# Second mixer of a two-block network: level products of a pair one projection later, first outputs earlier, turning on other banks

## The chip, the cores and the metric

The program runs on 1 core of a Trainium2 chip. The metric is the device time of one execution in microseconds (us). The kernel before took 1179.19 us, the median of three runs (1178.02, 1179.58, 1179.19).

## What is computed

Two networks run one after the other on 256 tokens of width 1024, all in float32 (matrix products as sums of three, see below). The change lies in the second one's first mixer, HGRN2:

```python
proj = h @ w_in
q, fl, v, g = jnp.split(proj, ...)          # 1024 wide each, 8 heads of 128
q = silu(q)
log_f = logaddexp(log(lb), log1p(-lb) + log_sigmoid(fl))
k = (1.0 - lb) * sigmoid(-fl)
# per head, over the 256 tokens: S_t = diag(f_t) S_{t-1} + k_t v_t^T, o_t = S_t^T q_t
o = o * rsqrt(mean(o * o) + EPS) * norm_w   # per head
o = o.reshape(B, S, 1024) * silu(g)
return o @ w_out
```

The kernel computes the scores q_t . decay(t, s) . k_s without a scan over tokens: the 256 tokens are cut in halves, those in halves, and so on. For each of the levels (blocks of 1, 2, 4 ... 128 tokens) `qT` and `kT` are multiplied in place by products of `f`, then one product `kT^T qT` gives the scores of all block pairs of that level, and a mask picks them out.

## The kernel before

**Weights.** All weights come as units of 128 x 2048 float32 (1 MB) through a ring of three buffers (`NS = 3`). Each unit is loaded by SyncE in two halves (`raw`, L2135), ScalarE rounds a half to `whi` (L958), VectorE subtracts to get `wlo` (L1369; in the feed-forward stages GpSimd does some, L1942), and TensorE multiplies three times: `whi` by `hh`, `wlo` by `hh`, `whi` by `hl` (L495, L498, L501 for outputs with columns on partitions; L512, L515, L518 for outputs by token). Both engines split two units ahead of the one that is being multiplied (`use`, in each engine's program). A load waits for the `wlo` of the unit three before.

**The order of the work** is written out by hand: each engine has its own program (`tensor_program`, `scalar_program`, `vector_program`, `gpsimd_program`, `sync_program`), each runs strictly in order, and they meet at semaphores. A bank of PSUM is taken by `turn(key, bank)`; `full`, `evac` and `free` name the waits for it. Banks 0 to 3 go round for projections, banks 4 to 7 (`4 + side[0] % 4`) for level products and the first outputs.

**The mixer.** The heads are worked in four pairs, j = 0 to 3. Units in order: `hf` 0, `hq` 0, `hf` 1, `hq` 1, ... `hq` 3 (forget and query columns of pair j, `project_columns`), then `hv` 0, `hg` 0, `hv` 1, `hg` 1 (values and gate of half the heads, by token, each in two units or parts, `project_tokens`), then `ho`, the output product (`add_product`).
- `f_of(j)`: VectorE scales the forget columns out of PSUM (L1416), ScalarE makes `kT` and `fT` by Sigmoid (L1212, L1213), VectorE finishes them (L1757, L1760). GpSimd then multiplies up the block products `tot` (`products(j)`, L2074).
- `q_of(j)`: VectorE scales the query columns (L1416), ScalarE makes `qT` by Silu (L1218).
- A level product (j, i), i = 0 to 8, is step i of pair j. On TensorE (`level`) it is four products of 128 x 128 x 128 (L857), two for i = 8 (L852); the trace has two records for each such product. It needs the bank, and for i = 0 `kT` and `qT` of pair j, for i > 0 the scaling of step i - 1. VectorE (`level` in its program) waits for the product, scales `qT` and `kT` for the next one (L1781, L1782; L1774 for i = 0), then copies the masked scores into `Ss` (L1787, `copy_predicated`). Step 8 is copied by ScalarE into `S01` (L1224).
- Which steps stand behind which projection is a table `LEVEL` made by `advance(key, pairs)`: each call takes the next step of each pair in `pairs` that has not had all nine. All engines read the same table (`levels(*key)`).
- `outputs(g2)`: for each half of the tokens (`tt`), scores times values (L879, and L878 with `S01` for the second half) into a bank, ScalarE squares it for the mean (L1245), VectorE and GpSimd make the root (L1799, L1949), VectorE multiplies by root and gate into `og` (L1804). ScalarE has made `sgt`, the Silu of the gate (L1239), and GpSimd multiplied it by the norm's weights (L2084, `scaled_gate`, two operations of 128 x 512 for each half of the heads).
- `turn_outputs(cs)`: transposes `og` (L889) into a bank; ScalarE copies `eh` (L1253), VectorE `el` (L1811), the operands of `ho`.

Before the change `outputs(0)` stands behind the second part of `hg` 0, and `turn_outputs((0, 1))` behind the last projection, on banks 0 and 1. The second half of the last gate projection is in bank 0.

Of the kernel before, what the change touches and what calls it, by code (L numbers as in the profile page):

```python
# [72 lines left out]
def build(nc, a):  # L73
    V, A, G, T, S = nc.vector, nc.scalar, nc.gpsimd, nc.tensor, nc.sync
    vq, aq, gq, tq, sq = Waits(V), Waits(A), Waits(G), Waits(T), Waits(S)
    with ExitStack() as root:
# [3 lines left out]
        def sbuf(ctx, name, shape, dt=f32):  # L80
            return ctx.enter_context(nc.sbuf_tensor(name, shape, dt))
# [62 lines left out]
        lev = sbuf(hg, "lev", [128, 8, 128], i32)  # L144
# [211 lines left out]
        def turn(key, b, fills=1):  # L356
            fills_of[b] += fills
            turns[key] = (b, evacuations[b], fills_of[b])
            evacuations[b] += 1
            return b  # L360
# [9 lines left out]
        def evac(*key):  # L370
            b, n, _ = turns[key]
            return s_evac[b], n + 1
# [76 lines left out]
        at_level, level_no, LEVEL = [0] * 4, {}, {}  # L449

        def advance(key, pairs):
            for j in pairs:
                if at_level[j] < 9:
                    LEVEL.setdefault(key, []).append((j, at_level[j]))
                    level_no[j, at_level[j]] = len(level_no) + 1
                    at_level[j] += 1

        for j in range(1, 4):
            advance(("hf", j), range(j))
            advance(("hq", j), range(j + 1))  # L460
        for g2 in range(2):
            for name in ("hv", "hg"):
                for part in range(2):
                    advance((name, g2, part), range(4))
            while min(at_level[2 * g2:2 * g2 + 2]) < 9:
                advance(("rest", g2), range(4))

        lev_q = {ji: i + 1 for i, ji in enumerate(ji for ji in sorted(level_no, key=level_no.get) if ji[1] < 8)}

# [7 lines left out]
        def tensor_program():  # L477
# [55 lines left out]
            def project_tokens(key, e, between=None):  # L533
                bs = [turn(("tok", *key, 0), next_bank()), turn(("tok", *key, 1), next_bank(), 2)]
                for part in range(2):
                    j = unit_at[(*key, part)]
                    for t in range(2):
                        if part == 0:
                            tq.wait_ge(*free(("tok", *key, t)))
                        tok = moving(banks[bs[t]][:, :], j, t, hh, hl, range(4 * part, 4 * part + 4), 0, 512, *of_norm(e),  # L540
                                     first=part == 0, last=part == 1)
                        if t == 1 or part == 1:
                            tok.then_inc(s_full[bs[t]], 1)
                    b, _, n = turns["tok", *key, 1]
                    used[j, 0] = used[j, 1] = (s_full[b], n - 1 + part)
                    if between is not None:
                        between(part)
# [77 lines left out]
            for t in range(2):  # L625
                for c in range(2):
                    b = turn(("tr", 0, 2 * t + c), 4 + 2 * t + c)
# [9 lines left out]
            wh, wl, b = whole(whi, 0), whole(wlo, 0), turns["col", "xbc", 0][0]  # L637
# [30 lines left out]
            j = unit_at["dtf",]  # L668
            b = turn(("dtf",), next_bank())
# [15 lines left out]
            for tt in range(2):  # L685
                b = turn(("xst", tt), 4 + tt)
# [5 lines left out]
            for g in range(2):  # L692
                b = turn(("cb", g), 6 + g)
# [166 lines left out]
            def levels(*key):  # L860
                for j, i in LEVEL.get(key, []):
                    level(j, i)

            def outputs(g2):
                for tt in range(2):
                    b = turn(("oo", g2, tt), 4 + side[0] % 4 if g2 == 0 else 2 + tt)
                    side[0] += 1
                    for j in (2 * g2, 2 * g2 + 1):
                        tq.wait_ge(*evac("lev", j, 7))
                        tq.wait_ge(*evac("lev", j, 8))  # L870
                    tq.wait_ge(*evac("tok", "hv", g2, 0))
                    tq.wait_ge(*evac("tok", "hv", g2, 1))
                    tq.wait_ge(*free(("oo", g2, tt)))
                    for i in range(4):
                        hd = 4 * g2 + i
                        vs, out = slice(128 * hd, 128 * hd + 128), banks[b][:, 128 * i:128 * i + 128]
                        if tt == 1:
                            T.matmul(out, S01[:, hd, :], vt[:, 0, vs], start=True, stop=False)  # L878
                        tok = T.matmul(out, Ss[:, 2 * hd + tt, :], vt[:, tt, vs], start=tt == 0, stop=True)  # L879
                    tok.then_inc(s_full[b], 1)  # L880

            def turn_outputs(cs):
                for c in cs:
                    b = turn(("tr", 4, c), c % 2)
                    tq.wait_ge(*free(("tr", 4, c)))
                    for t in range(2):
                        tq.wait_ge(*evac("oo", c // 2, t))
                        for k in range(2):
                            tok = T.transpose(banks[b][:, 256 * k + 128 * t:256 * k + 128 * t + 128],  # L889
                                              og[:, t, 256 * c + 128 * k:256 * c + 128 * k + 128], ident[:, :])  # L890
                    tok.then_inc(s_full[b], 1)

            project_pair([("hf", 0), ("hq", 0)], 3)
            for j in range(1, 4):
                project_columns(("hf", j), 3)
                levels("hf", j)
                project_columns(("hq", j), 3)
                levels("hq", j)
            for g2 in range(2):
                for name in ("hv", "hg"):  # L900
                    project_tokens((name, g2), 3, lambda part: levels(name, g2, part))
                if g2 == 0:
                    levels("rest", 0)
                    outputs(0)
            turn_outputs((0, 1))
            levels("rest", 1)
            outputs(1)
            add_product(("ho",), 4, eh, el, *of_norm(4), 5, before_last=lambda: turn_outputs((2, 3)))
            feed_forward(1, 5, 6)
# [37 lines left out]
        def scalar_program():  # L947
# [272 lines left out]
            def levels(*key):  # L1220
                for j, i in LEVEL.get(key, []):
                    if i == 8:
                        aq.wait_ge(*full("lev", j, 8))
                        A.activation(S01[:, 2 * j:2 * j + 2, :], bank_of("lev", j, 8)[:, 0:256].rearrange("p (h t) -> p h t", h=2),  # L1224
                                     ACT.Copy).then_inc(evacuated("lev", j, 8), 1)

            def tokens_of(name, g2):
                factors = (factor(3, 0), factor(3, 1))
                sl = slice(512 * g2, 512 * g2 + 512)
                for part in range(2):  # L1230
                    use((name, g2, part))
                    levels(name, g2, part)
                for t in range(2):
                    key = ("tok", name, g2, t)
                    aq.wait_ge(*full(*key))
                    if name == "hv":
                        A.activation(vt[:, t, sl], bank_of(*key)[:, :], ACT.Copy, scale=factors[t]).then_inc(evacuated(*key), 1)
                    else:
                        A.activation(sgt[:, t, sl], bank_of(*key)[:, :], ACT.Silu, scale=factors[t]).then_inc(evacuated(*key), 1)  # L1239

            def outputs(g2):
                for tt in range(2):
                    aq.wait_ge(*full("oo", g2, tt))
                    for i in range(4):
                        t = A.activation(hn[:, tt, 512 * g2 + 128 * i:512 * g2 + 128 * i + 128], bank_of("oo", g2, tt)[:, 128 * i:128 * i + 128],  # L1245
                                         ACT.Square, accum_out=mstat[:, 8 * tt + 4 * g2 + i:8 * tt + 4 * g2 + i + 1])
                    t.then_inc(s_osq, 1)
# [15 lines left out]
            for g2 in range(2):  # L1263
                tokens_of("hv", g2)
                tokens_of("hg", g2)
                if g2 == 0:
                    levels("rest", 0)
                    outputs(0)
            turn_outputs((0, 1))
            levels("rest", 1)  # L1270
            outputs(1)
            add_product(("ho",), 4, 5, before_last=lambda: turn_outputs((2, 3)))
            feed_forward(1, 5, 6)
# [83 lines left out]
        def vector_program():  # L1357
# [432 lines left out]
            def levels(*key):  # L1790
                for j, i in LEVEL.get(key, []):
                    level(j, i)
# [33 lines left out]
            for g2 in range(2):  # L1826
                for name in ("hv", "hg"):
                    for part in range(2):
                        use((name, g2, part))
                        levels(name, g2, part)  # L1830
                if g2 == 0:
                    levels("rest", 0)
                    outputs(0)
            turn_outputs((0, 1))
            levels("rest", 1)
            outputs(1)
            add_product(("ho",), 4, 5, before_last=lambda: turn_outputs((2, 3)))
            feed_forward(1, 5, 6)
# [350 lines left out]
```

## Time and profile before

| | us |
|---|---|
| median of three runs | 1179.19 |
| the profiled execution, its own time | 1177.87 |
| its span, first to last instruction | 1176.6 |
| TensorE matmul busy | 1142.4 (97%) |
| TensorE weight load busy | 1061.1 |
| VectorE busy | 670.1 |
| ScalarE busy | 583.0 |
| GpSimd busy | 295.9 |

The engines run beside one another; busy time is summed over an engine's own instructions, and matmuls are pipelined, so that a busy TensorE need not be at its peak. The mixer in question runs from about 540 to 694 us of the span. The mean granted clock of TensorE is 0.989 of full speed.

### The profile page before, as it was taken

To read this page: it belongs to the slowest core of one execution; us is meant where nothing else is said; L and a number is where in the kernel's file an instruction comes from. 1 tells how busy PE (TensorE), PEld (TensorE's weight loads), DVE (VectorE), ACT (ScalarE), POOL (GpSimd) and SP (SyncE) were. 2 spreads that over 40 slices of the span, in tenths; PEclk is the share of its full clock that TensorE was granted. 3 is DMA by queue.
4 is the path that set the end of the run, shared out by engine and by line. 5 is a ranking of instruction groups with operands and counts; after the bars stand their busy time and mean duration, and the time that the engine had idled before them with its cause. 6 is when DMAs were issued, how large, how long until landed. Compare 5 with 4: busy or idle time off the path is not lost.

```text
span 1176.6 us, 19533 instructions
## 1 busy us (share of the span) xinstructions
PE 1142.4 (97%) x8221; PEld 1061.1 (90%) x8221; DVE 670.1 (57%) x1043; ACT 583.0 (50%) x891; POOL 295.9 (25%) x191
## 2 busy tenths in 40 slices
PE   8999999999999999999899999999999869999997
PEld 6999989999989999889898889999889858999986
DVE  6555765577656454337897556334247785533424
ACT  6546555555436644337543444444345954544432
POOL 2023100000005444512321115444500001544440
PEclk9899999999999999999999999999999989999999
DMA  8669574545646666655443447655555534756550
GB/s 261 203 206 331 151 242 125 165 144 144 205 148 194 189 191 203 197 162 179 143 150 107 125 153 226 192 184 195 197 161 169 172 96 144 226 180 193 184 195 36
DMA packets 158257, 207.89 MB, mean 177 GB/s; under 512 B 13631, under 2 KB 131545, under 8 KB 158170
## 3 DMA queue, kind: packets, MB, share of 16 engines
q1 hardware_dynamic: 154442, 193.63, 52.8%
q0 software_dynamic: 3728, 13.02, 3.3%
q8 instruction: 65, 1.06, 0.4%
q14 instruction: 22, 0.18, 0.0%
HBM read 205.53 MB, written 4.24 MB: 178 GB/s over the span
## 4 chain that ended last, share of the span: by engine, by line
PE 88%; DVE 6%; ACT 3%; issue 1%; DMA 1%; POOL 0%; SPq 0%; DVEq 0%; ACTq 0%; POOLq 0%
PE bank L495 18%; PE bank L501 18%; PE bank L498 18%; PE bank L518 9%; PE bank L515 9%; PE bank L512 9%; DVE wlo L1369 2%; PE bank L857 2%; ACT whi L958 1%; PE bank L783 1%; PE bank L793 1%; DMA area<-in_hgrn_lb 1%; PE bank L805 1%; PE bank L558 1%; DVE uc L1499 0%
## 5 line engine op out<-in xcount | busy, mean ns | idle before, releaser
L1369 DVE TENSOR_TENSOR wlo<-raw,whi 128x1024 fp32r<-128x1024 f32 (+1 forms) x281 | 346.1, 1260 | 236.1 <-ACT whi L958 235.5
L958 ACT ACTIVATE whi<-raw 128x1024 fp32r<-128x1024 f32 x368 | 365.6, 1042 | 118.2 <-PE bank L518 112.6
L495 PE MATMUL bank<-hh,whi 128*128 128x256 f32 x1792 | 287.1, 281 | 1.7 <-ACT hh L990 1.7
L1942 POOL TENSOR_TENSOR wlo<-raw,whi 128x1024 fp32r<-128x1024 f32 x87 | 223.3, 2567 | 255.9 <-ACT whi L958 255.9
L501 PE MATMUL bank<-hl,whi 128*128 128x256 f32 x1792 | 282.6, 279 | 0.0
L498 PE MATMUL bank<-hh,wlo 128*128 128x256 f32 x1792 | 282.6, 279 | 0.0
L495 PEld LDWEIGHTS bank<-hh,whi 128*128 128x128 f32 x1792 | 242.4, 188 | 6.7 <-issue 5.5
L498 PEld LDWEIGHTS bank<-hh,wlo 128*128 128x128 f32 x1792 | 241.7, 188 | 0.0
L501 PEld LDWEIGHTS bank<-hl,whi 128*128 128x128 f32 x1792 | 241.7, 188 | 0.0
L1949 POOL TENSOR_TENSOR st<-st,half 128x1 f32<-128x1 f32 x18 | 10.3, 581 | 438.3 <-DVE st L1386 413.4
L512 PE MATMUL bank<-whi,gh 128*128 128x512 f32 x264 | 81.5, 390 | 0.0
L515 PE MATMUL bank<-wlo,gh 128*128 128x512 f32 x264 | 81.3, 389 | 0.0
L518 PE MATMUL bank<-whi,gl 128*128 128x512 f32 x264 | 81.3, 389 | 0.0
L1186 ACT ACTIVATE sg<-sg 128x512 f32<-128x512 f32 x33 | 20.9, 632 | 95.6 <-DVE sg L1416 95.6
L1190 ACT ACTIVATE gh<-sg 128x512 fp32r<-128x512 f32 x33 | 20.8, 631 | 85.9 <-DVE sg L1730 85.9
L518 PEld LDWEIGHTS bank<-whi,gl 128*128 128x128 f32 x264 | 49.6, 188 | 10.4
L515 PEld LDWEIGHTS bank<-wlo,gh 128*128 128x128 f32 x264 | 49.6, 188 | 10.3
L512 PEld LDWEIGHTS bank<-whi,gh 128*128 128x128 f32 x264 | 49.2, 188 | 9.9
L1730 DVE TENSOR_TENSOR sg<-sg,bank 128x512 f32<-128x512 f32 x33 | 22.7, 687 | 57.5 <-PE bank L501 55.4
L1416 DVE TENSOR_TENSOR sg<-bank,bc_f 128x512 f32<-128x512 f32 x33 | 22.7, 688 | 43.9 <-PE bank L501 43.9
L983 ACT ACTIVATE bank<-x_sb 128x512 f32<-128x512 f32 x28 | 16.8, 599 | 57.1 <-DVE x_sb L1438 29.9
L1732 DVE TENSOR_TENSOR gl<-sg,gh 128x512 fp32r<-128x512 f32 x33 | 30.8, 932 | 23.3 <-ACT gh L1190 23.3
(306 smaller groups left out, 1281.1 us busy)
## 6 DMA issues: line engine op xcount, KB each, us to landing
raw<-in_ffn_w_in SPq DMA_DIRECT2D x88, 512.0 KB, 3.6
raw<-in_w_in SPq DMA_DIRECT2D x72, 512.0 KB, 4.7
raw<-in_ffn_w_out SPq DMA_DIRECT2D x44, 512.0 KB, 3.4
raw<-in_hgrn_w_in SPq DMA_DIRECT2D x32, 512.0 KB, 4.3
raw<-in_w_ffn_gate SPq DMA_DIRECT2D x22, 512.0 KB, 4.4
raw<-in_w_ffn_up SPq DMA_DIRECT2D x22, 512.0 KB, 4.1
raw<-in_w_ffn_down SPq DMA_DIRECT2D x22, 512.0 KB, 3.3
raw<-in_w_branch SPq DMA_DIRECT2D x16, 512.0 KB, 4.3
```

Source lines behind the costliest of these rows:

```text
L495: T.matmul(out, wh[:, i, c], xh[:, k, :], start=first and (i, k) == pairs[0], stop=False)
L498: T.matmul(out, wl[:, i, c], xh[:, k, :], start=False, stop=False)
L501: t = T.matmul(out, wh[:, i, c], xl[:, k, :], start=False, stop=last and (i, k) == pairs[-1])
L512: T.matmul(out, xh[:, k, r], wh[:, i, c], start=first and i == 0, stop=False)
L515: T.matmul(out, xh[:, k, r], wl[:, i, c], start=False, stop=False)
L518: tok = T.matmul(out, xl[:, k, r], wh[:, i, c], start=False, stop=last and i == len(ks) - 1)
L857: tok = T.matmul(banks[b][:, 128 * (2 * h + t):128 * (2 * h + t) + 128], kj[:, h, c], qj[:, h, c], start=True, stop=True)
L958: A.activation(half_of(whi, j, h), half_of(raw, j, h), ACT.Copy).then_inc(s_hi[j % NS][h], 1)
L1369: V.tensor_tensor(half_of(wlo, j, h), half_of(raw, j, h), half_of(whi, j, h).bitcast(f32), ALU.subtract).then_inc(s_lo[j % NS][h], 1)
L1416: V.tensor_tensor(dst, two(bank_of("col", *key)[:, :]), bc[:, :].rearrange("p (o t) -> p o t", o=1).broadcast_to([128, 2, 256]), ALU.mult) ...
L1732: V.tensor_tensor(gl[:, 2 * j:2 * j + 2, :], two(s), gh[:, 2 * j:2 * j + 2, :].bitcast(f32), ALU.subtract).then_inc(s_gl, 1)
L1942: G.tensor_tensor(half_of(wlo, j, 1), half_of(raw, j, 1), half_of(whi, j, 1).bitcast(f32), ALU.subtract).then_inc(s_lo[j % NS][1], 1)
```

## The change

The four parts of it: pair j's level step behind `hq` j is left out there, so that each pair j from 1 on starts one projection later; `outputs(0)` moves from behind `hg` 0 to behind the first part of `hv` 1, on all engines; the first turning goes to banks 6 and 7; what is left of the levels, one product (3,8), is issued on TensorE behind that turning, on ScalarE ahead of its copies of it. An assertion says that pairs 0 and 1 are done where the first outputs now stand.

```diff
         for j in range(1, 4):
             advance(("hf", j), range(j))
-            advance(("hq", j), range(j + 1))
+            advance(("hq", j), range(j))
         for g2 in range(2):
             for name in ("hv", "hg"):
                 for part in range(2):
                     advance((name, g2, part), range(4))
-            while min(at_level[2 * g2:2 * g2 + 2]) < 9:
-                advance(("rest", g2), range(4))
+                    assert (name, g2, part) != ("hv", 1, 0) or min(at_level[0:2]) == 9
+        while min(at_level) < 9:
+            advance(("rest",), range(4))
...
                     for j in (2 * g2, 2 * g2 + 1):
                         tq.wait_ge(*evac("lev", j, 7))
-                        tq.wait_ge(*evac("lev", j, 8))
+                        if tt == 1:
+                            tq.wait_ge(*evac("lev", j, 8))
...
-                    b = turn(("tr", 4, c), c % 2)
+                    b = turn(("tr", 4, c), 6 + c if c < 2 else c - 2)
...
+            def behind(name, g2, part):
+                levels(name, g2, part)
+                if (name, g2, part) == ("hv", 1, 0):
+                    outputs(0)
+
             for g2 in range(2):
                 for name in ("hv", "hg"):
-                    project_tokens((name, g2), 3, lambda part: levels(name, g2, part))
-                if g2 == 0:
-                    levels("rest", 0)
-                    outputs(0)
+                    project_tokens((name, g2), 3, lambda part: behind(name, g2, part))
             turn_outputs((0, 1))
-            levels("rest", 1)
+            levels("rest")
             outputs(1)
...
             for g2 in range(2):
                 tokens_of("hv", g2)
                 tokens_of("hg", g2)
-                if g2 == 0:
-                    levels("rest", 0)
-                    outputs(0)
+            levels("rest")
             turn_outputs((0, 1))
-            levels("rest", 1)
             outputs(1)
```

(The second hunk of the last pair is ScalarE's; VectorE's program changes as TensorE's does.) The level table, written as (pair, step):

| behind | before | now |
|---|---|---|
| `hf` 1 | 0,0 | 0,0 |
| `hq` 1 | 0,1 1,0 | 0,1 |
| `hf` 2 | 0,2 1,1 | 0,2 1,0 |
| `hq` 2 | 0,3 1,2 2,0 | 0,3 1,1 |
| `hf` 3 | 0,4 1,3 2,1 | 0,4 1,2 2,0 |
| `hq` 3 | 0,5 1,4 2,2 3,0 | 0,5 1,3 2,1 |
| `hv` 0, parts 0 and 1 | 0,6 1,5 2,3 3,1; 0,7 1,6 2,4 3,2 | 0,6 1,4 2,2 3,0; 0,7 1,5 2,3 3,1 |
| `hg` 0, parts 0 and 1 | 0,8 1,7 2,5 3,3; 1,8 2,6 3,4 | 0,8 1,6 2,4 3,2; 1,7 2,5 3,3 |
| `hv` 1, parts 0 and 1 | 2,7 3,5; 2,8 3,6 | 1,8 2,6 3,4; 2,7 3,5 |
| `hg` 1, parts 0 and 1 | 3,7; 3,8 | 2,8 3,6; 3,7 |
| rest | none | 3,8 |

TensorE behind the projection `hq` 1, before: the end of that projection in bank 0, the level products (0,1) in bank 5 and (1,0) in bank 6, the start of `hf` 2 in bank 1.

```order
L501 MATMUL bank0<-hl,whi 128x256 x4
L857 MATMUL bank5<-qT,kT 128x128 x4
L857 MATMUL bank6<-qT,kT 128x128 x4
L495 MATMUL bank1<-hh,whi 128x256 x4
L498 MATMUL bank1<-hh,wlo 128x256 x4
```

The same place now (lines have moved by one), up to the end of `hf` 2 and what stands behind it:

```order
L502 MATMUL bank0<-hl,whi 128x256 x4
L858 MATMUL bank5<-qT,kT 128x128 x4
L496 MATMUL bank1<-hh,whi 128x256 x4
L499 MATMUL bank1<-hh,wlo 128x256 x4
...
L502 MATMUL bank1<-hl,whi 128x256 x4
L858 MATMUL bank6<-qT,kT 128x128 x4
L858 MATMUL bank7<-qT,kT 128x128 x4
```

(1,0) is gone from behind `hq` 1; it is the second of the two behind `hf` 2.

TensorE at the end of the mixer, before: (3,7) in bank 4, the last projection's second part in banks 3 and 0, (3,8) in bank 5, the turning, the second outputs, the output product.

```order
L857 MATMUL bank4<-qT,kT 128x128 x4
...
L518 MATMUL bank0<-whi,hl 128x512 x4
L852 MATMUL bank5<-qT,kT 128x128 x2
L889 MATMUL bank0<-ident,og 128x128 x4
L889 MATMUL bank1<-ident,og 128x128 x4
L879 MATMUL bank2<-vt,Ss 128x128 x4
...
L512 MATMUL bank4<-whi,eh 128x512 x2
```

And now:

```order
L519 MATMUL bank0<-whi,hl 128x512 x4
L858 MATMUL bank4<-qT,kT 128x128 x4
L891 MATMUL bank6<-ident,og 128x128 x4
L891 MATMUL bank7<-ident,og 128x128 x4
L853 MATMUL bank5<-qT,kT 128x128 x2
L881 MATMUL bank2<-vt,Ss 128x128 x4
...
L513 MATMUL bank4<-whi,eh 128x512 x2
```

(3,7) has moved from ahead of the last part to behind it, and the turning, on other banks, now stands between (3,7) and (3,8).

ScalarE there, before:

```order
L1224 ACTIVATE S01<-bank5 128x256
L1239 ACTIVATE sgt<-bank3,st 128x512
L1239 ACTIVATE sgt<-bank0,st 128x512
L1253 ACTIVATE eh<-bank0 128x512
L1253 ACTIVATE eh<-bank1 128x512
```

And now:

```order
L1245 ACTIVATE sgt<-bank3,st 128x512
L1245 ACTIVATE sgt<-bank0,st 128x512
L1228 ACTIVATE S01<-bank5 128x256
L1259 ACTIVATE eh<-bank6 128x512
L1259 ACTIVATE eh<-bank7 128x512
```

The copy of (3,8) has moved from ahead of the gate's Silu to behind it.

## Rows read from the trace of the kernel before

**Rows 1.** The page, part 1: busy us (share of the span) xinstructions.

```profile
PE 1142.4 (97%) x8221; PEld 1061.1 (90%) x8221; DVE 670.1 (57%) x1043; ACT 583.0 (50%) x891; POOL 295.9 (25%) x191
```

**Rows 2.** Who waited for whom, TensorE, 540 to 694 us: us in total, times, longest.

```profile
PE bank L857 <- ACT qT L1218: 3.1, 1, 3.1
...
PE bank L889 <- ACT sgt L1239: 1.6, 1, 1.6
```

**Rows 3.** Timeline around `hq` 1 and 2: start us, us, engine, line [idle before].

```profile
560.90 1.16 PE L857 MATMUL bank<-qT,kT 128*128 128x128 f32 x8 [0.20 <-DVE qT L1774]
564.36 0.63 ACT L1218 ACTIVATE qT<-qT 128x512 f32<-128x512 f32 x1 [2.21 <-DVE qT L1416]
565.13 1.13 PE L857 MATMUL bank<-qT,kT 128*128 128x128 f32 x8 [3.08 <-ACT qT L1218]
566.02 0.72 PE L495 MATMUL bank<-hh,whi 128*128 128x256 f32 x4
...
579.19 1.95 PE L857 MATMUL bank<-qT,kT 128*128 128x128 f32 x16
581.40 1.13 PE L857 MATMUL bank<-qT,kT 128*128 128x128 f32 x8 [0.26 <-issue]
```

**Rows 4.** Timeline of VectorE: its wait behind `hf` 2, the last projection's split.

```profile
571.95 0.69 DVE L1416 TENSOR_TENSOR fT<-bank,bc_hg 128x512 f32<-128x512 f32 x1 [2.06 <-PE bank L501]
...
647.82 2.37 DVE L1369 TENSOR_TENSOR wlo<-raw,whi 128x1024 fp32r<-128x1024 f32 x2
```

**Rows 5.** Timeline of TensorE at the end of the mixer's products.

```profile
657.48 1.05 PE L857 MATMUL bank<-qT,kT 128*128 128x128 f32 x8
658.28 1.18 PE L512 MATMUL bank<-whi,hh 128*128 128x512 f32 x4
...
663.97 0.60 PE L852 MATMUL bank<-qT,kT 128*128 128x128 f32 x4
666.21 1.09 PE L889 MATMUL bank<-ident,og 128*128 128x128 f32 x8 [1.63 <-ACT sgt L1239]
667.14 1.06 PE L879 MATMUL bank<-vt,Ss 128*128 128x128 f32 x8
...
669.74 0.71 PE L512 MATMUL bank<-whi,eh 128*128 128x512 f32 x2
```

**Rows 6.** Timeline of ScalarE and GpSimd, same place.

```profile
664.61 0.38 ACT L1224 ACTIVATE S<-bank 128x256 f32<-128x256 f32 x1 [4.87 <-PE bank L852]
664.89 1.26 ACT L1239 ACTIVATE sgt<-bank,st 128x512 f32<-128x512 f32 x2
665.65 2.50 POOL L2084 TENSOR_TENSOR sgt<-sgt,nw 128x512 f32<-128x512 f32 x2 [23.75 <-ACT sgt L1239]
```

**Rows 7.** Timeline of VectorE behind level product (3,7).

```profile
658.57 0.43 DVE L1781 TENSOR_TENSOR qT<-qT,tot 128x256 f32<-128x256 f32 x1 [2.51 <-PE bank L857]
658.91 0.42 DVE L1782 TENSOR_TENSOR kT<-kT,tot 128x256 f32<-128x256 f32 x1
659.24 0.74 DVE L1787 COPY_PREDICATED Ss<-lev,bank 128x512 f32<-128x512 int32 x1
```

**Rows 8.** Timeline of GpSimd and VectorE, 634 to 638 us.

```profile
634.31 2.82 POOL L2084 TENSOR_TENSOR sgt<-sgt,nw 128x512 f32<-128x512 f32 x2 [26.96 <-ACT sgt L1239]
634.50 1.49 DVE L1782 TENSOR_TENSOR kT<-kT,tot 128x256 f32<-128x256 f32 x1
...
636.56 0.85 DVE L1781 TENSOR_TENSOR qT<-qT,tot 128x256 f32<-128x256 f32 x1
...
637.67 0.74 DVE L1787 COPY_PREDICATED Ss<-lev,bank 128x512 f32<-128x512 int32 x1
```

**Rows 9.** Timeline of GpSimd and VectorE, 574 to 577 us.

```profile
574.94 1.33 POOL L2074 TENSOR_TENSOR tot<-fT 128x256 f32<-128x256 f32 x1 [9.54 <-DVE fT L1757]
...
575.38 0.42 DVE L1782 TENSOR_TENSOR kT<-kT,tot 128x256 f32<-128x256 f32 x1
```

**Rows 10.** TensorE in a window: window, us, busy (x), granted clock, DMA share, GB/s.

```profile
925.00:930.00 5.00, 5.00 (x32) 0.66 0.65 201
```

More of the change, by code:

```diff
@@ L1232, in tokens_of @@
                     levels(name, g2, part)
+                    if (name, g2, part) == ("hv", 1, 0):
+                        outputs(0)
                 for t in range(2):
@@ L1830, in vector_program @@
                         levels(name, g2, part)
-                if g2 == 0:
-                    levels("rest", 0)
-                    outputs(0)
+                        if (name, g2, part) == ("hv", 1, 0):
+                            outputs(0)
             turn_outputs((0, 1))
-            levels("rest", 1)
+            levels("rest")
             outputs(1)
```

## The prediction

> **What bounds the kernel.** I read the busy line first: TensorE is busy 97% of the span [rows 1], so a change can only pay where TensorE stands still. The list of who waits for whom, over the second mixer (540 to 694 us), shows the few places. The reader is to see two large waits: 3.1 us of a level product for ScalarE's `qT`, and 1.6 us of the turning for ScalarE's `sgt` [rows 2]. In the timeline [rows 3] the first wait stands at 565.13. ScalarE's Silu of pair 1's `qT` runs from 564.36 for 0.63 us, and the level product that has to have it is pair 1's step 0, issued right behind the projection that made that same `qT`. A small wait of the same kind, on pair 2's step 0, stands at 581.40. The second large wait is at 666.21, where the turning wants bank 0, and bank 0 is held by the last gate tile until ScalarE has read it [rows 5, 6].
>
> How TensorE's time is counted: these matmuls follow one another at a fixed spacing. Eight records of a level product take 0.89 us (565.13 to 566.02), so one takes 0.111 [rows 3]. I measure a wait from start to start, not by the idle time, which leaves out the drain.
>
> **Part 1: level products of a pair one projection further back.** Nothing is added or removed: every product, scaling and masked copy is still there. Step (1,0) leaves the end of `hq` 1 and goes behind `hf` 2; (2,0) leaves `hq` 2; (3,0) leaves `hq` 3.
> - At `hq` 1, (0,1) starts at 560.90 and its eight records end at 561.79; (1,0) starts at 565.13 [rows 3]. TensorE now goes on to `hf` 2 at 561.79. Saved: 565.13 - 561.79 = **3.34 us**. (1,0) comes when `hf` 2 is done, 5.9 us later (566.02 to 571.95, where VectorE sees it finished [rows 3, 4]), at 567.7, and its `qT` is there at 565.0: 2.7 us to spare.
> - At `hq` 2, sixteen records from 579.19 end at 580.97, and (2,0) starts at 581.40 [rows 3]. Saved: **0.43 us**.
> - At `hq` 3 no wait is seen; I count nothing.
>
> Does something else come late? TensorE reaches the end of `hf` 2 4.23 us earlier (3.34, and 0.89 of work put off). VectorE waited 2.06 us for it there [rows 4], and it also sheds (1,0): its two operations and a wait before them, near 1.8 us. So VectorE starts pair 2's forget gate about 0.4 us late. That delays only scalings whose products TensorE issues a whole projection later. From there VectorE's work is unchanged in amount: per projection a 2.35 us split, 0.69 for the scaled copy, 1.3 for each step (its row of three operations [rows 7]). With four steps that is about 8.2 us against 5.9 + 3.6 of TensorE. It stays within one projection of TensorE. Weights: the split for the last projection ended at 650.19 (647.82 + 2.37) and is used from 658.28 on [rows 4, 5]. It now stands behind the first outputs in VectorE's queue, but those come earlier too. I cost the supply at nothing; the cover is these 8 us.
>
> **Part 2: first outputs inside the second value projection.** The 24 records of `outputs(0)` (2.60 us, as between 667.14 and 669.74 [rows 5]) move past one projection. No wait stood before them, and none follows: their banks 6 and 7 are the same. Cost 0. What is queued behind them: ScalarE's and VectorE's splits for the last projection. The moved piece's own DMAs: none; the load queue waits for splits alone, and keeps its order.
>
> **Part 3: the end.** Before, with start-to-start times [rows 5]: (3,7) at 657.48, last projection 658.28 to 663.97, (3,8) 0.44 us, wait to 666.21 (1.80 us), turning 0.93, outputs 2.60, product from 669.74. Now (3,7) stands behind the last projection. Call its start T = 663.97 - 0.80 = 663.17 (less the savings of part 1).
> - (3,7) ends at T + 0.80, the turning on banks 6 and 7 has nothing to wait for (those banks were read out a projection ago), and ends at T + 1.73.
> - (3,8) needs pair 3's `qT` and `kT` scaled after (3,7). Undisturbed, VectorE starts `qT` 1.09 after the product's start (658.57 against 657.48), ends `kT` at 1.85 and the masked copy at 2.50 [rows 5, 7]. Then (3,8) starts at T + 1.91, outputs (which need that copy) at T + 2.56, and the `ho` product at T + 5.16 = 668.33. Saved: 1.41.
> - But GpSimd now scales the gate in the same moment. ScalarE reads a tile 0.20 after its last matmul (664.41 to 664.61), takes 0.63, and GpSimd follows 0.13 later [rows 5, 6]: its second operation holds from about T + 0.96 for 1.3 us, to T + 2.3. When the same operations met before [rows 8], `kT` took 1.49 instead of 0.42; the next `qT`, started inside the second operation, 0.85. That second operation ended near 637.13 (634.31 + 2.82), and the masked copy at 638.41, 1.28 behind it. So here the masked copy ends at T + 3.6, outputs start at T + 3.66, and the product at T + 6.27 = 669.44. Saved: **0.30**.
>
> What else is queued there: ScalarE copies (3,8) into `S01` ahead of the two `eh` copies, since its program has the rest in front of the turning. `S01` is wanted by the second output tile, 0.9 us after the first starts, `eh` by the `ho` product, 2.6 us after. Both are in time in either case: the copy of (3,8) follows within 0.7 us of its start (663.97 to 664.61) and takes 0.38 [rows 5, 6].
>
> The bounds of this part are 1.41 and 0.30; I take 0.30, since rows 8 are the same two instructions. Against it stand [rows 9]: there `kT` took 0.42 with a GpSimd operation open since 574.94. VectorE was in unbroken work there; at T it is idle and GpSimd comes first. The Trainium skill (SBUF — State Buffer, Who interferes with whom) says that a VectorE instruction with two inputs in SBUF and a GpSimd instruction that reads SBUF shut one another out, and that whoever starts first has the ports for its whole instruction. It speaks against this change; rows 8 agree, and by it the term is 0.30, without it 1.41.
>
> **Sum.** 3.34 + 0.43 + 0.30 = 4.07 us. The profiled execution took 1177.87 (span 1176.6 and 1.3 around it), which gives 1173.8. The median of the three runs, 1179.19, stands 1.32 higher, so I predict 1179.19 - 4.07 = **1175.1 us**. Two medians of this kernel can be told apart from about 0.2%, 2.4 us (the runs spread over 1.6).
>
> **Rivals.**
> - *GpSimd does not hold VectorE up at the end.* For it: rows 9. Against it: rows 8. Saved 3.34 + 0.43 + 1.41 = 5.18: 1174.0. Chance 0.21.
> - *VectorE takes the place of ScalarE.* It has little idle time in the mixer, and TensorE now comes over 4 us earlier. If VectorE's scalings fell a whole projection behind, the waits of part 1 would come back at later level products, releaser VectorE; what is left is the end and a bit, up to 0.8: 1178.4. For it: the 2.06 us of slack is used up. Against it: scalings are wanted one projection after they can start, and one step costs 1.3 against 5.9. Chance 0.13.
> - *The clock falls (slower).* Place: the end of the mixer, where the one wait of 1.80 becomes two shorter ones around (3,8). In 925 to 930 us the granted clock is 0.66, so part of it ran at 1.2 GHz, and that cost (1 - 0.66) x 5 = 1.7 us; TensorE had been waiting in the 10 us before [rows 10]. It decides from 13 us at 1.2 GHz on: 6.5 us lost, 4.07 gained, 1181.6. Against it: the wait is shorter in sum than the one of before, after which no fall was seen. Chance 0.04.
>
> **The numbers.** The forecast has 0.62. Faster by over 0.2% are the forecast, the first rival and 0.02 of the second: 0.85. Within 0.2%: 0.12, the rest of the second and 0.01 of the third. Slower: 0.03. Range: the first rival's 1174.0 less 1.2 for the scatter of runs, 1172.8; above, the forecast plus one fall of the clock like that at 925 us that lands otherwise (1.7) and 0.6 of scatter, 1177.4.
>
> **What would show it.** Right: no wait of a level product for `qT` of ScalarE near 562; `hf` 2 starts right behind (0,1); no wait of the turning for `sgt`; instead (3,8) and the first of the last outputs wait over 1 us each or together for VectorE, with a `qT` or `kT` scaling of 1 us or more beside GpSimd's `sgt`. Half right: those scalings at 0.42 and a gain near 5. Wrong: waits of level products for VectorE inside the mixer, or a wait for weights (`wlo`) at the last two projections.

## The result and the profile after

| | before | after |
|---|---|---|
| median, us | 1179.16 (4 runs, 1178.02 to 1179.58) | 1172.36 (4 runs, 1171.19 to 1174.49) |
| ratio | | 0.9943 [0.9928, 0.9959] |
| profiled execution, its own time | 1177.87 | 1171.74 |
| its span | 1176.6 | 1170.5 |
| mean granted clock | 0.989 | 0.992 |

Faster by 6.8 us (0.6%), where 4.07 was predicted; the time lies 0.4 us below the range. Over all executions of this study the difference is smaller: before 1179.49 (median of 79), after 1173.63 (median of 17, the four above among them), 5.86 us apart.

The busy line of the page of the kernel after, against [rows 1]:

```profile
PE 1139.9 (97%) x8221; PEld 1059.0 (90%) x8221; DVE 669.8 (57%) x1043; ACT 583.0 (50%) x891; POOL 294.9 (25%) x191
```

No engine has less to do: the same 8221 matmul records, the same 1043, 891 and 191 instructions. What went is standing still. Who waited for whom in the kernel after, TensorE, 540 to 694 us (us in total, times, longest), against [rows 2]:

```profile
PE bank L853 <- DVE kT L1785: 1.0, 1, 1.0
...
PE bank L513 <- ACT eh L1259: 0.3, 1, 0.3
PE bank L858 <- DVE qT L1777: 0.2, 1, 0.2
```

The 3.1 us of a level product for ScalarE's `qT` and the 1.6 of the turning for `sgt` are not there. One new wait stands in their place: 1.0 us of (3,8) for VectorE's `kT`.

The timeline of the kernel after behind `hq` 1, against [rows 3, 4] (start us, us, engine, line [idle before]):

```profile
559.01 1.16 PE L858 MATMUL bank<-qT,kT 128*128 128x128 f32 x8 [0.17 <-DVE qT L1777]
...
559.93 0.72 PE L496 MATMUL bank<-hh,whi 128*128 128x256 f32 x4
...
562.48 0.63 ACT L1222 ACTIVATE qT<-qT 128x512 f32<-128x512 f32 x1 [2.22 <-DVE qT L1419]
...
565.67 1.95 PE L858 MATMUL bank<-qT,kT 128*128 128x128 f32 x16
...
566.37 0.68 DVE L1419 TENSOR_TENSOR fT<-bank,bc_hg 128x512 f32<-128x512 f32 x1
```

`hf` 2 starts 0.92 behind (0,1), where before 5.12 lay between them (560.90 to 566.02). (1,0) is now the second half of the sixteen records at 565.67; its `qT` was done at 563.11 (562.48 + 0.63), 2.6 us ahead of the first of them. VectorE takes up pair 2's forget columns at 566.37 with no idle time before it: its slack of 2.06 is gone, as the prediction had it. In before it took up the same columns 0.20 behind the start of the level products (571.95 and 571.75), here 0.70 behind it (566.37 and 565.67), so it is 0.5 us late; 0.4 was predicted. One pair later it waits for TensorE again:

```profile
580.75 0.69 DVE L1419 TENSOR_TENSOR fT<-bank,bc_hg 128x512 f32<-128x512 f32 x1 [0.91 <-PE bank L502]
```

The timeline of the kernel after at the end of the mixer, against [rows 5 to 7]:

```profile
657.38 1.05 PE L858 MATMUL bank<-qT,kT 128*128 128x128 f32 x8
657.58 0.69 ACT L1245 ACTIVATE sgt<-bank,st 128x512 f32<-128x512 f32 x1 [2.11 <-PE bank L519]
...
658.26 1.04 PE L891 MATMUL bank<-ident,og 128*128 128x128 f32 x8
658.34 1.27 POOL L2086 TENSOR_TENSOR sgt<-sgt,nw 128x512 f32<-128x512 f32 x1 [1.52 <-ACT sgt L1245]
658.47 1.42 DVE L1784 TENSOR_TENSOR qT<-qT,tot 128x256 f32<-128x256 f32 x1 [2.83 <-PE bank L858]
659.81 0.41 DVE L1785 TENSOR_TENSOR kT<-kT,tot 128x256 f32<-128x256 f32 x1
660.15 0.72 DVE L1790 COPY_PREDICATED Ss<-lev,bank 128x512 f32<-128x512 int32 x1
...
660.28 0.71 PE L853 MATMUL bank<-qT,kT 128*128 128x128 f32 x4 [0.98 <-DVE kT L1785]
...
660.92 1.16 PE L881 MATMUL bank<-vt,Ss 128*128 128x128 f32 x8
...
663.62 0.70 PE L513 MATMUL bank<-whi,eh 128*128 128x512 f32 x2
```

With T = 657.38: GpSimd's gate operation starts at T + 0.96, 0.13 ahead of VectorE's scaling of `qT`, and that takes 1.42 instead of 0.43 [rows 7]. (3,8) starts at T + 2.90, the outputs at T + 3.54 (predicted 3.66), the `ho` product at T + 6.24 (predicted 6.27).

**What the old wait consisted of.** [rows 2] name ScalarE as the releaser, but ScalarE itself had waited 2.21 us for VectorE's scaled copy [rows 3]. VectorE's timeline in before shows why that came late:

```profile
561.39 2.33 DVE L1369 TENSOR_TENSOR wlo<-raw,whi 128x1024 fp32r<-128x1024 f32 x2
563.65 0.67 DVE L1416 TENSOR_TENSOR qT<-bank,bc_hg 128x512 f32<-128x512 f32 x1
```

The split of a weight unit stands ahead of the scaled copy of `hq` 1 in VectorE's program, though that projection was done by about 560.9. Had the copy stood ahead of the split, it would have come 2.3 us sooner (561.39 for 563.65), and of the wait, 3.3 us from start to start, about 1.1 would have been left; that is an estimate from these rows, and no run tried it. The change goes round the wait and leaves this order in place.

**Where the time came from.** I cut each trace at the start of (0,1), the last thing ahead of the change, and at the start of the `ho` product. Before: 560.90 and 669.74, so 108.84 us of mixer. After: 559.01 and 663.62, so 104.61. Difference 4.23. What lies behind the cut is alike (506.86 and 506.88 to the end of the span). The other 1.9 us of the two profiled executions lie ahead of (0,1), where both programs are the same. So the first question was whether the missing 2 to 3 us are chance, or a part of the change that one trace does not show.

### The profile page after: what moved, and what is told of

Its sections match the earlier page's. It is cut to its first block, busy times and chain, and to the rows that moved or that the text cites. A ratio compares the mean times of both kernels' runs of the same rounds, so it can differ in the third digit from the quotient of the medians.

```text
span 1170.5 us, 19533 instructions
## 1 busy us (share of the span) xinstructions
PE 1139.9 (97%) x8221; PEld 1059.0 (90%) x8221; DVE 669.8 (57%) x1043; ACT 583.0 (50%) x891; POOL 294.9 (25%) x191
## 4 chain that ended last, share of the span: by engine, by line
PE 89%; DVE 6%; ACT 3%; issue 1%; DMA 1%; POOL 0%; SPq 0%; DVEq 0%; ACTq 0%; POOLq 0%
PE bank L496 18%; PE bank L502 18%; PE bank L499 18%; PE bank L513 9%; PE bank L519 9%; PE bank L516 9%; PE bank L858 2%; DVE wlo L1372 2%; ACT whi L962 1%; PE bank L784 1%; PE bank L794 1%; PE bank L806 1%; PE bank L559 1%; DMA area<-in_hgrn_lb 1%; DVE uc L1502 0%
```

## The experiments

The theory at this point: 4.23 us by the waits, the rest scatter. The rival: some executions of before lose more at the waits than its first trace shows, since the granted clock falls behind them.

**More traces and runs of both kernels.** `same_before` and `same_after` are the two kernels unchanged.

> The kernel before, unchanged, measured against itself. Theory A (the 2.6 us by which the measured gain, 6.8 us, exceeds the 4.23 us that the mixer saves in the trace is chance: the granted clock falls once or twice in the first 60 us and in the rglru stage, for a time that differs from run to run): ratio 1.000, single executions 3 us or more apart, with mean clocks that go with their times. Rival B (the rest is a property of the two programs): the executions of this kernel all lie within 1178 to 1180 us and none comes near 1176.

> The changed kernel, unchanged, measured again. Theory A: a gain of 4.2 us, with 1 us of scatter (ratio 0.9964). Rival B: 6.8 us again (ratio 0.9943).

Measured: before 1179.36 (12 runs), ratio 1.0 [0.9989, 1.0012]; after 1173.76 (6 runs), ratio 0.9952 [0.9937, 0.9967]. The single executions of before spread from 1177.85 to 1183.32 here, those of after from 1173.23 to 1176.84, and the medians lie 5.6 apart: neither 4.2, as the first of the two theories has it, nor 6.8. The mixer of `same_after` took 104.61, to the hundredth what it took the first time. That of `same_before` took 110.37, 1.53 more than in the first trace. The windows view of TensorE in `same_before` shows where (window, us, busy (x), granted clock, DMA share, GB/s):

```profile
560.00:565.00 5.00, 1.75 (x13) 1.00 0.40 135
565.00:568.00 3.00, 3.00 (x17) 0.57 0.56 186
568.00:571.00 3.00, 3.00 (x24) 0.86 0.34 109
571.00:575.00 4.00, 4.00 (x37) 1.00 0.53 181
```

And the first trace of before, same stretch:

```profile
565.00:568.00 3.00, 2.87 (x25) 1.00 0.71 246
568.00:571.00 3.00, 3.00 (x28) 1.00 0.32 79
```

TensorE had stood still for 3.08 us. Then it worked with a granted clock of 0.57 over 3 us, so nearly all of it at the lower level, 1.2 GHz. The timeline of `same_before` shows it in the spacing of the records:

```profile
564.85 1.52 PE L857 MATMUL bank<-qT,kT 128*128 128x128 f32 x8 [3.08 <-ACT qT L1218]
566.03 1.20 PE L495 MATMUL bank<-hh,whi 128*128 128x256 f32 x4
567.02 1.05 PE L498 MATMUL bank<-hh,wlo 128*128 128x256 f32 x4
```

and the first trace of before, the same two groups of records:

```profile
566.02 0.72 PE L495 MATMUL bank<-hh,whi 128*128 128x256 f32 x4
566.57 0.63 PE L498 MATMUL bank<-hh,wlo 128*128 128x256 f32 x4
```

From start to start the four records of L495 take 0.99 there and 0.55 here. The Trainium skill (TensorE: Matmul & The Clock Gate, Part 1: The HAM clock gate) says of the start of a kernel that the point at which the clock changes is not tied to the kernel and differs from run to run. The two traces of one program, 1.00 and 0.57 behind the same wait, agree in that the place of the kernel does not decide it.

**How often?** Four more traces of before, and one more timed run of after.

> One more trace of the kernel before, unchanged. Theory (the clock falls behind the 3.1 us wait of (1,0) in about half of the executions): the stretch from (0,1) to the ho product is either 108.8 us with granted clock 1.00 throughout 565 to 571 us, or near 110.4 with a window under 1. Nothing in between, and no fall elsewhere in the mixer.

> One more trace of the kernel before. Theory: 108.8 us from (0,1) to the ho product with the clock at 1.00, or 110.4 with a fall in the 5 us behind the wait of (1,0); the start of (0,1) anywhere from 559 to 566 us, set by how long the clock is down between 40 and 50 us.

> As the run before it: 108.8 or 110.4 us in the mixer, the start of (0,1) between 559 and 566 us, and 506 to 507.5 us from the ho product to the end.

> A sixth trace of the kernel before, on the same chip as the filled kernel. Theory: 108.8 us without a fall, 110.3 to 111.2 with one behind the wait of (1,0); nothing else in the mixer differs.

> The changed kernel, unchanged, once more. Theory (4.23 us from the waits in every execution, about 0.6 us on average from the fall of the clock that no longer follows the wait of (1,0), and the rest of the first 6.8 us chance of the first 560 us): 4.2 to 5.5 us faster than before over many executions, 104.6 us from (0,1) to the ho product, no fall in the mixer. Rival (the program as a whole gains 6 to 7 us, from something outside the mixer): 6 to 7 us, and the stretch before the mixer or the one behind it shorter than in the traces of before.

| trace | mixer, us | granted clock in the 12 us behind (0,1) |
|---|---|---|
| before, first | 108.84 | 1.00 |
| same_before | 110.37 | 0.86 |
| look_before2 | 108.79 | 1.00 |
| look_before3 | 111.19 | 0.72 |
| look_before4 | 110.34 | 0.86 |
| look_before5 | 110.36 | 0.86 |
| after, same_after, same_after2 | 104.61 each | 1.00 each |

The clock falls in four of six executions of before, at a cost of 1.50 to 2.35 us over the 108.84, and in none of three of after. The mean of the six is 109.98, so the change is worth 109.98 - 104.61 = **5.37 us** in the mixer: 4.23 of waits and 1.14 of clock. (`look_before3`, with 111.19, lies outside what was expected of a fall, 110.4; the fall there began with (1,0) itself, whose eight records took 1.70 instead of 0.89.) `same_after2`: 1173.48 (7 runs), ratio 0.9954 [0.9938, 0.997].

**Is it the standing still that brings the fall?** In the kernel before, TensorE fills the wait of (1,0) with 14 products of the identity (28 records), into the bank that (1,0) then overwrites. The wait for `qT` stays.

```diff
+                if (j, i) == (1, 0):
+                    tq.wait_ge(*free(("lev", j, i)))
+                    for _ in range(14):
+                        T.matmul(banks[b][:, 0:128], ident[:, :], ident[:, :], start=True, stop=True)
                 if i == 0:
                     tq.wait_ge(s_k, j + 1)
```

> The kernel before, with fourteen products of ident by ident issued ahead of level product (1,0) into the bank that it overwrites: TensorE works through the wait for qT, and (1,0) starts no sooner. Theory (the fall of the clock comes from TensorE standing still for 3 us, in 4 of the 7 traces that have the wait, and costs 1.5 to 2.4 us each): no fall, 108.8 us from (0,1) to the ho product, and a median about 1 us under the kernel before (1.07 on average over the five traces of before). Rival (the falls in these traces have nothing to do with the wait): windows under 1.00 here too, and no difference in the times.

> The same kernel with the wait filled, a second trace. Theory: 108.8 us again, granted clock 1.00 in the 12 us behind (0,1). Rival: 110 us or more in some of the three traces.

> The same kernel with the wait filled, a third trace. Theory: 108.8 us again, granted clock 1.00 in the 12 us behind (0,1).

The timeline of `f1_wait_filled`:

```profile
562.05 1.16 PE L861 MATMUL bank<-qT,kT 128*128 128x128 f32 x8 [0.17 <-DVE qT L1778]
563.04 3.29 PE L847 MATMUL bank<-ident 128*128 128x128 f32 x28
566.30 1.13 PE L861 MATMUL bank<-qT,kT 128*128 128x128 f32 x8
```

(1,0) starts 4.25 behind (0,1), as in before (4.23): the filling delays nothing and saves nothing by itself. In its three traces the mixer took 108.60, 108.80 and 108.84, the granted clock 1.00 each time. Of all traces with the 3.1 us of standing still, those of the next two experiments among them, five of eight show the fall; of the ten without it, none. The three traces of the filled wait alone would be weak evidence (`look_before5`, on the same chip, fell, but two of the six traces of before did not); the ten and eight together are what it rests on. Timed: 1178.39 (12 runs), ratio 0.999 [0.9976, 1.0004]; that is 1.1 below the 1179.49 of before, by medians, as the mean cost of the clock (1.14) asks for. The interval alone does not settle a gain of that size; the traces do.

**The two parts apart.** `u1_pair1_back` puts pair 1's steps back where they were, `t1_end_alone` all steps, so that of the change only the places of the outputs and the turning with its banks are left:

```diff
-            advance(("hq", j), range(j))
+            advance(("hq", j), range(max(j, 2)))
```

```diff
-            advance(("hq", j), range(j))
+            advance(("hq", j), range(j + 1))
```

> The changed kernel, but pair 1 alone begins behind hq 1 again; pairs 2 and 3 stay a projection later. Theory (the saving of part 1 is the wait of (1,0) for ScalarE's qT, 3.34 us, and beside it a fall of the granted clock behind that wait in some executions, which cost 1.53 us in one of two traces of the kernel before): the wait of 3.1 us is back, the stretch from (0,1) to the ho product is 104.61 + 3.34 = 107.95 us, or 109.5 if the clock falls, and the kernel is 3.3 to 5 us slower than the changed one. Rival (VectorE's backlog would have taken part of it back, so that the wait is worth less than its length): under 2.5 us slower.

> The level table of before in full, with the outputs and the turning where the change put them: the parts at the end alone. Theory: the turning no longer waits for sgt, (3,8) is ahead of it as before, so 1.80 us are saved and nothing else: 107.04 us from (0,1) to the ho product (108.84 before), plus 1.5 if the clock falls behind the wait of (1,0); 1.8 us faster than before. Rival (the first outputs inside hv 1 cost something that the pairs' shift hid): less than 1 us.

The timeline of `u1_pair1_back` has the old wait again, at its old length:

```profile
564.15 1.16 PE L858 MATMUL bank<-qT,kT 128*128 128x128 f32 x8 [0.19 <-DVE qT L1777]
568.39 1.13 PE L858 MATMUL bank<-qT,kT 128*128 128x128 f32 x8 [3.08 <-ACT qT L1222]
```

Its mixer took 107.71, 3.10 more than after's (no fall in this trace); its time was 1179.02 (12 runs), ratio 0.9999 [0.9985, 1.0012], so 5.4 above after's, more than wait and clock explain (3.1 and 1.1) and more than the 3.3 to 5 that was expected. The 1.2 left over are less than the interval of this run allows for (about 1.6 to either side), and no trace shows a cause of them. `t1_end_alone`: mixer 108.48 with a fall of the clock. From (0,1) to the products behind `hf` 2 it took 12.40 us, where the first trace of before took 10.85 (560.90 to 571.75), so the fall cost 1.55 and the mixer would be 106.93 without it, 1.9 less than before. Its time, 1178.95 (12 runs), ratio 0.9996 [0.9983, 1.0009], can't confirm that: the interval reaches from no gain to one of 2.0.

**What the end is made of.** `g1_gate_op_waits` holds GpSimd's last gate operation back until VectorE has scaled `qT` and `kT` for (3,8). `b1_old_banks` gives the turning its old banks.

```diff
                     gq.wait_ge(s_hgw, 32)
+                    if g2 == t == 1:
+                        gq.wait_ge(s_q, lev_q[3, 7])
```

```diff
-                    b = turn(("tr", 4, c), 6 + c if c < 2 else c - 2)
+                    b = turn(("tr", 4, c), c % 2)
```

> The changed kernel, in which GpSimd's last gate operation also waits for VectorE's scaling behind level product (3,7). Theory (GpSimd's operation shuts VectorE's scaling out, 1.42 us instead of 0.43 in the trace of the changed kernel): that scaling takes 0.43, the wait of (3,8) falls from 0.98 to under 0.1 us, and the kernel is 1.0 to 1.1 us faster than the changed one; from the start of (3,7) to the ho product 5.2 us instead of 6.24. Rival (the scaling is slow for another reason, or the wait only moves to the outputs or to the root, which needs the gate): no difference, 6.2 us in that stretch.

> The changed kernel with the first turning on banks 0 and 1 again. Theory: it then waits for ScalarE's last sgt, which ends 0.89 us after (3,7) starts, against 0.80 for (3,7) itself; the turning starts 0.1 us later, and (3,8) waits for VectorE longer than that anyway: 104.6 us, no difference from the changed kernel, so the banks are worth nothing here. Rival: the banks carry the saving at the end; 1 us slower or more.

The timeline of `g1_gate_op_waits`, the same place as above:

```profile
661.89 1.05 PE L858 MATMUL bank<-qT,kT 128*128 128x128 f32 x8
...
662.98 0.42 DVE L1784 TENSOR_TENSOR qT<-qT,tot 128x256 f32<-128x256 f32 x1 [2.83 <-PE bank L858]
663.32 0.42 DVE L1785 TENSOR_TENSOR kT<-kT,tot 128x256 f32<-128x256 f32 x1
...
663.79 0.71 PE L853 MATMUL bank<-qT,kT 128*128 128x128 f32 x4
663.88 1.27 POOL L2088 TENSOR_TENSOR sgt<-sgt,nw 128x512 f32<-128x512 f32 x1 [2.53 <-DVE kT L1785]
...
667.14 0.71 PE L513 MATMUL bank<-whi,eh 128*128 128x512 f32 x2
```

The scaling is back at 0.42, (3,8) starts at T + 1.90 and the product at T + 5.25 (661.89 to 667.14), 0.99 earlier than in after; the mixer took 103.62. Only GpSimd's start was changed, so it was GpSimd's operation that held VectorE up. By time 1172.96 (6 runs), ratio 0.9939 [0.9924, 0.9955]: 0.7 below after's pooled median, less than these runs tell apart.

In `b1_old_banks` the mixer took 104.62, so the banks by themselves are worth nothing:

```profile
658.65 1.05 PE L858 MATMUL bank<-qT,kT 128*128 128x128 f32 x8
659.59 1.09 PE L891 MATMUL bank<-ident,og 128*128 128x128 f32 x8
661.56 0.71 PE L853 MATMUL bank<-qT,kT 128*128 128x128 f32 x4 [0.87 <-DVE kT L1785]
```

Since (3,7) now stands between the gate projection and the turning, bank 0 is read out almost in time: the turning starts 0.94 behind (3,7) instead of 0.88, and the wait of (3,8) shrinks from 0.98 to 0.87. Its time was 1173.57 (12 runs), ratio 0.9958 [0.9944, 0.9972].

**Pair 3 kept where it was.** Pair 3 had no wait to lose, and its chain is the one that ends last. `c1_pair3_kept` delays pairs 1 and 2 only:

```diff
-            advance(("hq", j), range(j))
+            advance(("hq", j), range(j + j // 3))
```

> The changed kernel, but pair 3 begins behind hq 3 as before, so that (3,8) is behind the last projection and nothing is left for after the turning. Theory: pair 3 never waited for its qT (it is ready 0.2 us before TensorE comes to it), so nothing is lost there, and the whole 1.80 us wait of before at the turning is gone with no new one behind it: 1.3 us faster than the changed kernel, 5.6 us faster than the kernel before in the trace of the mixer. Rival (ScalarE's copy of (3,8) and the gate's Silu ahead of the eh copies hold the ho product up, or pair 3's step 0 waits now that TensorE comes 4 us earlier): under 0.5 us, with a wait for eh, el or qT in the list.

> The kernel with pair 3 kept behind hq 3, once more, in one call with the changed kernel. Theory: 103.17 us from (0,1) to the ho product, 1.4 us less than the changed kernel; the medians 1 to 2 us apart in its favour. Rival: the difference in the times was chance and the two are equal.

(3,7) is now hidden behind the first part of the last projection, and the timeline of `c1_pair3_kept` has no wait left at the end:

```profile
664.65 0.60 PE L853 MATMUL bank<-qT,kT 128*128 128x128 f32 x4
665.09 1.04 PE L891 MATMUL bank<-ident,og 128*128 128x128 f32 x8
665.97 1.06 PE L881 MATMUL bank<-vt,Ss 128*128 128x128 f32 x8
...
668.56 0.70 PE L513 MATMUL bank<-whi,eh 128*128 128x512 f32 x2
```

Its mixer took 103.17 in both traces, 1.44 less than after's. By the starts of after, 1.13 of that stood ahead of (3,8) (the turning's 0.89 end at 659.15, (3,8) starts at 660.28), 0.20 between (3,8) and the outputs (0.64 instead of 0.44), 0.11 in the outputs (2.70 instead of 2.59). Timed: 1172.51 (6 runs), ratio 0.994 [0.9923, 0.9957], and 1172.55 (6), 0.9942 [0.9927, 0.9957]. Together 1172.55 against 1173.63 for after: the direction of the traces, though times alone do not separate the two. Of all versions run this has the shortest mixer and the lowest pooled median, though `g1_gate_op_waits` (103.62; 1172.96) is too near to be told apart by time. The two together were not tried.

## Why the prediction was right and wrong

**Right: the places and what releases them.** No level product waits for ScalarE's `qT`, the turning does not wait for `sgt`, and the one new wait is that of (3,8) for VectorE. Part 1 can be read from starts in the two first traces, counted from (0,1). The products behind `hq` 2 start at 18.29 before (579.19 - 560.90) and at 14.10 after (573.11 - 559.01), with one level product (0.89) less ahead of them: the first wait gave 4.19 - 0.89 = 3.30, predicted 3.34. Those behind `hf` 3 start at 27.13 before (588.03) and at 21.54 after (580.55), with two products (1.78) less ahead of them: 3.81 in all, so the second wait gave 0.51, predicted 0.43. That leaves 4.23 - 3.81 = 0.42 for the end, predicted 0.30; the difference is for the most part that (3,7) took 0.88 in after, and the prediction went by its 0.80 before. `u1_pair1_back` puts 3.10 on the first wait instead of 3.30: in its `hf` 2 four records take 0.453 us where the other traces have 0.471, 0.2 over the projection. What brings that is open.

**Right: the lock at the end.** The choice between 0.30 and 1.41 was the one judgement in the sum, made by [rows 8] against [rows 9]. The scaling took 1.42, and 0.42 once GpSimd came behind it. The rule of the Trainium skill (SBUF — State Buffer, Who interferes with whom) that spoke against this change holds here. Why the two did not hold one another up in [rows 9] stays open.

**Right: nothing else came late.** VectorE's backlog did not reach TensorE, the weights came in time, and the clock stayed up behind the waits of the end (granted clock 1.00 in after from 655 to 670 and from 670 to 694 us). Those rivals fell. That the turning would have nothing to wait for on banks 6 and 7 was right too, but the banks are not the cause: on the old ones it waits less than 0.1.

**Wrong: the size, by one missing term.** The step that failed is "Saved: 565.13 - 561.79 = 3.34 us". It took the wait at the length that one trace shows, and what follows the wait at nothing. The length was right (3.30), but behind this wait of 3.1 us the granted clock fell in four of six executions of before, and what TensorE did next then ran at 1.2 GHz for some us: 1.14 us in the mean of six. In the trace I read the clock happened to stay at 1.00, and I looked for falls only as something the change could bring (the slower rival) and as scatter, not as something it takes away. The trace it read had a sign of it: the fall at 925 us [rows 10], which the prediction used as a price, stands behind waits of TensorE of 1.16 and 2.30 us (they end at 920.02 and 923.98), shorter than the one that it removed. With the measured terms the sum is 3.81 + 0.42 + 1.14 = 5.37, and the time 1179.19 - 5.37 = 1173.8, inside the range; the pooled median of after is 1173.63.

**The rest is scatter, and it pushed the first result out of the range.** (0,1) starts anywhere from 559.01 to 565.39 us in the 18 traces of this study, though all run the same program up to there (before 560.61 to 564.21, after 559.01 to 561.65, variants of after up to 565.39). Its mean is 562.0 in the nine traces of before and of the filled wait, and 562.5 in the nine of after and its variants, so the 1.9 us by which the two first traces differ there are chance. The four first executions of after came out at 1172.36, the thirteen later ones at 1173.69; by the pooled median the time would have been inside the range, though 1.5 below the forecast. I had allowed 1.2 us for scatter below the lowest case, and that case lacked the 1.14. What stays open is the difference between 5.37 in the mixer and 5.86 by medians, which is within what these medians scatter.

## What to carry to other kernels

A long wait of TensorE costs its length plus what the clock does behind it, and one trace can miss the second part: look at the granted clock behind a long wait in several executions before pricing its removal. Follow the wait back past the engine that it names: here ScalarE was named, and by the rows 2.3 us of it lay in a split that stood ahead in VectorE's program. Move a product past the wait of its operand, but leave alone the chain that ends last: pair 3 had no wait, and delaying it too cost 1.44 us. Where a GpSimd operation on SBUF can start in the same moment as a short VectorE scaling that TensorE waits for, let it start behind the scaling; that turned 1.42 us back into 0.42.

## What the runs showed of the hardware that I had not expected

- After 3.08 to 3.09 us of standing still, the same program kept a granted clock of 1.00 in some executions and fell to the 1.2 GHz level in others (five of eight traces); the cost was 1.50 to 1.55 us in four and 2.35 in one.
- Much earlier in the program, with TensorE busy throughout, the clock falls too. In the timeline of before, products only 16 columns wide begin:

```profile
36.84 0.95 PE L512 MATMUL bank<-whi,hh 128*128 128x16 f32 x8
```

In the windows view of before, behind it:

```profile
40.00:45.00 5.00, 5.00 (x25) 0.60 0.67 205
45.00:50.00 5.00, 5.00 (x17) 0.72 0.62 182
```

and of after, the same code:

```profile
40.00:45.00 5.00, 5.00 (x24) 0.66 0.53 175
45.00:50.00 5.00, 5.00 (x23) 1.00 0.81 241
```

How long it lasts differs between executions. By these rows after had (0.06 + 0.28) x 5 = 1.7 us more of full clock, most of the 1.9 by which the two first traces differ ahead of the mixer. Whether the narrow products bring the fall was not tried.
- A head start of 0.13 us was enough for a GpSimd operation of 1.27 us to hold up a VectorE scaling that takes 0.42 alone: that ended at 659.89, 0.28 behind GpSimd's end at 659.61. The trace of after has a second case, off TensorE's path: a scaling at 625.33 took 1.44 beside GpSimd's gate operation, which had started at 625.21.
